# The opening of a two-layer trunk in four even blocks of granules, with eight modulation buffers

## The chip, the cores and the metric

One Trainium2 chip; the kernel runs on one of its cores. The metric is the device time of one execution in microseconds (us), the median of several runs; lower is better. A profiled execution gives the trace from which all rows here come. Engines are named as in the trace: PE is TensorE, DVE VectorE, ACT ScalarE, POOL GpSimd, SP SyncE, which only issues transfers.

## What is computed

A batch of one sequence of 256 tokens, width 2048, float32, goes through two layers. Each layer takes its input, normalizes it, scales and shifts it by a modulation that depends on a condition vector, and adds a gated branch:

```python
cond = jax.nn.silu(c)
for layer in range(DEPTH):                                  # 2
    mod = cond @ ada_w[layer] + ada_b[layer]                # 2048 x 6144 of weights
    shift, scale, gate = jnp.split(mod, 3, axis=-1)
    h = rms_norm(x, norm_w[layer]) * (1.0 + scale[:, None, :]) + shift[:, None, :]
    y = moba_branch(...) if layer % 2 == 0 else mlstm_branch(...)
    x = x + gate[:, None, :] * y
```

Layer 0 is attention: `proj = h @ w_in` gives q, k, v and z of 2048 columns each (16 heads of 128), q and k are normalized and rotated, the attention within one block of 256 tokens is causal, and `(o * silu(z)) @ w_out` is the branch. Layer 1 is an mLSTM of 8 heads. The change concerns the start of layer 0 alone.

## The kernel before

**Precision.** Every weight tile is split on the chip into a high and a low part, and so is h; a product is three matmuls, hi x hi, lo x hi, hi x lo. ACT writes the high part of a weight tile (`hi`, L546, w_hi<-raw), DVE the rest (`lo`, L822, w_lo<-raw,w_hi).

**Granules.** The unit of work on PE is a granule: 256 rows of the contraction (two of 128) by 512 columns of weights, against all 256 tokens. It is 12 matmuls of 128x512 (L1315 to L1317) and uses one weight tile of 512 KB. Tiles lie in LEAD = 5 slots of `raw`, `w_hi`, `w_lo`. A granule is (unit, group, r): the unit is Q, K, V, Z or the output projection O, the group is one of four groups of four heads, r = 0 to 7 is the place in the contraction. Granule r needs the parts 2r and 2r+1 of h, of 16.

**Order.** `ORDER0` lists layer 0's granules. PE runs them in this order; ACT and DVE run the same list with "places": at place i they prepare the tile of granule i + 5 and then do the tasks that a table has for place i (in some tables, `z_copy`, `z_add`, the tasks stand ahead of the preparation). SP issues at place i the load of granule i + 5 and then the modulation tiles that `TAKES0` has for place i. All queues run strictly in order.

**Modulation.** Of layer 0's shift and scale, 16 tiles of 512 KB (128 x 2 x 512) make a block, and four blocks (`b` = 0 to 3) make all; block b yields the modulation of h's parts 4b to 4b+3, thus of r = 2b and 2b+1. A tile is loaded into one of four buffers of `ada_raw` (`load_ada`, L478) and multiplied into a sum by DVE (`take_ada`, L841, a "take"). After 16 takes PE adds up over the partitions (`mod_sum`, L1434, "sum 0" to "sum 3"; it writes bank 3 of `mix`), ACT writes shift and scale (`mod_evac0`, L582 and L585) and makes h: high part L601 and full h L606, two of each for one r (`h_make`); DVE makes the low part (`h_rest`, L887, h_lo). Later tiles (layer 1 and the gates) use the same buffers.

**The opening.** Since h appears in four pieces while the modulation is loaded, the first 56 granules are in four blocks (`BLOCKS0`): 14 with r = 0 and 1, 10 with r = 2 and 3, 16 with r = 2 to 5, and 16 with the rest. To have enough work, the blocks also hold z of groups 0 to 2 and v of group 1 ("z parts"). Q and K of group 0 stay in PSUM banks of their own and V in `mix` 0 and 1; in the first three blocks all z parts take turns in banks 2 and 3 of `mix`. When a part's run in a block ends, ACT copies the bank (`z_copy`, L613) or, if there is a copy from before, DVE adds it (`z_add`, L857). A granule that needs the bank waits for that (`claim0`). Sums 1 to 3 stand behind granules 10, 21 and 36 (`SUM_AFTER`), the last takes of their blocks at places 8, 20 and 35.

**Before the first granule.** SP issues 16 modulation tiles; the four pieces of x come behind tiles 3 (two pieces), 4 and 5. ACT squares x, DVE adds up behind its tenth take, POOL makes the power, ACT and DVE scale x (L566, L873), PE transposes it into eight banks, ACT copies them (L576), and only then PE does sum 0.

The semaphore waits that matter below:

```python
wait(sp, ada_tile, n - ADA_SLOTS + 1)          # load_ada: the buffer's last tile must be taken
wait(sp, lo_ready, number(it, c) - LEAD + 1)   # load_raw
pe.wait_ge(xnT_act, UNIT)                      # ahead of sum 0: all eight banks copied
```

## Time and profile before

| | |
|---|---|
| median of 3 runs | 1515.51 us (1514.44 to 1517.66) |
| the profiled execution | 1514.53 us |
| its span, first to last instruction | 1512.7 us |
| PE busy | 1449.8 us, 96% |
| DVE busy | 1104.8 us, 73% |
| ACT busy | 750.5 us, 50% |
| DMA | 361.47 MB, mean 239 GB/s |
| first granule starts | 46.45 us |

Busy shares are means over the whole span. The opening, up to about 178 us, is another regime than the rest: it is there that the modulation is loaded beside the weights. A duration in the trace is that of one instruction; on PE the next one starts before the last has ended, so the work of a granule is read from the starts. A bracket is idle time of the engine ahead of an instruction, and what ended it.

### The profile page before, as it was taken

To read this page: it belongs to the slowest core of one execution; us is meant where nothing else is said; L and a number is where in the kernel's file an instruction comes from. 1 tells how busy PE (TensorE), PEld (TensorE's weight loads), DVE (VectorE), ACT (ScalarE), POOL (GpSimd) and SP (SyncE) were. 2 spreads that over 40 slices of the span, in tenths; PEclk is the share of its full clock that TensorE was granted. 3 is DMA by queue.
4 is the path that set the end of the run, shared out by engine and by line. 5 is a ranking of instruction groups with operands and counts; after the bars stand their busy time and mean duration, and the time that the engine had idled before them with its cause. 6 is when DMAs were issued, how large, how long until landed. Compare 5 with 4: busy or idle time off the path is not lost.

```text
span 1512.7 us, 19059 instructions
## 1 busy us (share of the span) xinstructions
PE 1449.8 (96%) x6679; PEld 1200.8 (79%) x6679; DVE 1104.8 (73%) x1224; ACT 750.5 (50%) x1024; POOL 42.3 (3%) x78
## 2 busy tenths in 40 slices
PE   2889999999999989999999999999999999999998
PEld 2767888888888867778888888888888888888886
DVE  5889799989989786887866566566666666656657
ACT  3554546455445545645544554454454554454552
POOL 1000010001000000010000000000000000000000
PEclk9899999999999999999999999999999999999999
...
GB/s 312 376 364 367 313 297 339 305 343 269 330 302 351 283 131 181 215 339 289 260 179 193 170 193 184 176 193 182 172 192 191 167 192 190 172 184 193 179 181 112
DMA packets 199230, 361.47 MB, mean 239 GB/s; under 512 B 14224, under 2 KB 48360, under 8 KB 199164
## 3 DMA queue, kind: packets, MB, share of 16 engines
...
q10 hardware_dynamic: 1056, 1.06, 0.2%
...
q14 instruction: 25, 0.20, 0.0%
...
## 4 chain that ended last, share of the span: by engine, by line
PE 76%; issue 9%; DVE 6%; DMA 4%; ACT 3%; SPq 0%; POOL 0%; ACTq 0%; DVEq 0%; POOLq 0%
PE proj L1315 23%; PE proj L1317 22%; PE proj L1316 22%; DVE ada_acc L841 3%; DMA raw<-in_att_w_in 3%; DMA ada_raw<-in_ada_w 2%; PE mix L1315 1%; PE mix L1316 1%; PE mix L1317 1%; DVE w_lo L822 1%; ACT w_hi L546 1%; PE mix L1434 1%; PE mix L1501 1%; PE mix L1549 1%; ACT work L634 1%
## 5 line engine op out<-in xcount | busy, mean ns | idle before, releaser
L822 DVE TENSOR_TENSOR w_lo<-raw,w_hi 128x1024 fp32r<-128x1024 f32 x480 | 586.1, 1223 | 362.2 <-ACT w_hi L546 361.1
L546 ACT ACTIVATE w_hi<-raw 128x1024 fp32r<-128x1024 f32 x480 | 507.8, 1061 | 683.6 <-PE proj L1317 577.5
L1315 PE MATMUL proj<-w_hi,h_hi 128*128 128x512 f32 x1472 | 585.0, 397 | 8.6 <-DVE h_lo L887 5.7
L1317 PE MATMUL proj<-w_hi,h_lo 128*128 128x512 f32 x1472 | 575.7, 391 | 0.0
L1316 PE MATMUL proj<-w_lo,h_hi 128*128 128x512 f32 x1472 | 575.5, 391 | 0.0
L1315 PEld LDWEIGHTS proj<-w_hi,h_hi 128*128 128x128 f32 x1472 | 278.0, 189 | 69.2 <-DVE h_lo L887 6.0
L1317 PEld LDWEIGHTS proj<-w_hi,h_lo 128*128 128x128 f32 x1472 | 277.7, 189 | 58.9
L1316 PEld LDWEIGHTS proj<-w_lo,h_hi 128*128 128x128 f32 x1472 | 278.1, 189 | 57.9 <-issue 1.4
L841 DVE SCALAR_TENSOR_TENSOR ada_acc<-ada_raw,cond,ada_acc 128x1024 f32<-128x1024 f32 x180 | 230.3, 1279 | 10.2 <-DMA ada_raw<-in_ada_w 8.6
L1315 PE MATMUL proj<-w_hi,y_hi 128*128 128x512 f32 x320 | 126.0, 394 | 1.3 <-DVE stream L985 1.3
L1317 PE MATMUL proj<-w_hi,y_lo 128*128 128x512 f32 x320 | 124.6, 389 | 0.0
L1316 PE MATMUL proj<-w_lo,y_hi 128*128 128x512 f32 x320 | 124.5, 389 | 0.0
L1315 PEld LDWEIGHTS proj<-w_hi,y_hi 128*128 128x128 f32 x320 | 60.1, 188 | 14.3 <-DVE stream L985 1.5
L1316 PEld LDWEIGHTS proj<-w_lo,y_hi 128*128 128x128 f32 x320 | 60.1, 188 | 12.8 <-issue 0.5
L1317 PEld LDWEIGHTS proj<-w_hi,y_lo 128*128 128x128 f32 x320 | 60.1, 188 | 12.6
L1315 PE MATMUL mix<-w_hi,h_hi 128*128 128x512 f32 x128 | 51.0, 398 | 4.9 <-issue 4.9
L1316 PE MATMUL mix<-w_lo,h_hi 128*128 128x512 f32 x128 | 50.3, 393 | 0.0
L1317 PE MATMUL mix<-w_hi,h_lo 128*128 128x512 f32 x128 | 50.3, 393 | 0.0
L991 DVE TENSOR_TENSOR ada_raw<-proj,gate 128x1024 f32<-128x1024 f32 x32 | 39.0, 1218 | 5.5 <-PE proj L1317 5.5
L1037 DVE SCALAR_TENSOR_TENSOR work<-work,conv_c 128x256 f32<-128x256 f32 x96 | 40.0, 480 | 0.0
L994 DVE TENSOR_TENSOR stream<-ada_raw,stream 128x1024 f32<-128x1024 f32 x32 | 39.2, 1226 | 1.1
L1315 PEld LDWEIGHTS mix<-w_hi,h_hi 128*128 128x128 f32 x128 | 24.5, 191 | 11.4 <-issue 6.5
(201 smaller groups left out, 902.1 us busy)
## 6 DMA issues: line engine op xcount, KB each, us to landing
...
raw<-in_att_w_in SPq DMA_DIRECT2D x128, 512.0 KB, 7.5
raw<-in_mlstm_w_in SPq DMA_DIRECT2D x128, 256.0 KB, 3.0
...
```

The costliest lines, as they stand in the source:

```text
L546: act.activation(w_hi[:, c % LEAD, :], raw[:, c % LEAD, :], ACT.Copy).then_inc(hi_ready, 1)
L634: op = act.activation(dump0[:, t, h], ps[:, t, h * HD:(h + 1) * HD], ACT.Square, accum_out=qk_ss[:, i:i + 1])
L822: dve.tensor_tensor(w_lo[:, c % LEAD, :], raw[:, c % LEAD, :], w_hi[:, c % LEAD, :].bitcast(F32), ALU.subtract).then_inc(lo_ready, 1)
L841: dve.scalar_tensor_tensor(out=sum_, in0=w, scalar=cond[:, t:t + 1], in1=other, op0=ALU.mult, op1=ALU.add).then_inc(ada_tile, 1)
L991: dve.tensor_tensor(scaled, both[q % 2][:], gate_both(q), ALU.mult).then_inc(out_part, 1)
L994: dve.tensor_tensor(x_q, scaled, x_q, ALU.add).then_inc(out_evac, 1)
L1037: op = dve.scalar_tensor_tensor(out=cv[:, j, :], in0=src, scalar=w, in1=cv[:, j, :], op0=ALU.mult, op1=ALU.add)
L1315: pe.matmul(out_, a_hi, b_hi, start=start, stop=False, **kw)
L1316: pe.matmul(out_, a_hi, b_lo, start=False, stop=False, **kw)
L1317: return pe.matmul(out_, a_lo, b_hi, start=False, stop=stop, **kw)
L1434: op = pe.matmul(mix[bank][:, j:j + 1], ada_acc[:, which, j // 4, j % 4 * P:(j % 4 + 1) * P], ones[:, 0:1], start=True, stop=True)
L1501: op = pe.transpose(mix[2 + f // 2][:, (f % 2) * SEQ + t * P:(f % 2) * SEQ + (t + 1) * P], y[:, t, f * P:(f + 1) * P], ident)
```

## The change

- `BLOCKS0`: four blocks of 14 granules. Block b has r = 2b and 2b + 1 alone, of q, k, v, of z of groups 0 to 2 and of v of group 1. The middle two are written by `middle0`. The sums now stand behind granules 10, 25 and 39, the last takes at places 8, 23 and 37.
- The z parts are thus ended in all four blocks: one copy and three additions each, 12 additions in place of 9 (8 of them ahead of granule 42, where 5 stood ahead of granule 40). The second block begins with a z granule.
- Modulation tiles of layer 0 have eight buffers: four of `ada_raw`, two of a new tensor in space that later tensors of layer 0 use, and two in `work`. To clear that space, `conv_rows` lies in `raw`, and SP waits for its transposes ahead of the first weight tile. From the fifth block on there are four buffers again.
- x is queued one tile earlier (behind tiles 3 and 4).
- `mod_evac0` on ACT (five instructions) is gone; DVE's `mod_evac` (two) does it. For the first r DVE writes the full h (`by_both`) while ACT writes the high part.
- `h_rest` stands ahead of `lo` at its two places, not behind it. Sum 0 waits for four copied banks, not eight.
- The evacuations of q, k, v of group 0 come two places later (43, 45, 47) and so does its attention; it keeps its distance to them.

```diff
+ADA_START = 8
+def middle0(r):
+    both = (r, r + 1)
+    return (unit0(Z_, 0, both) + [(Q_, 0, r)] + unit0(Z_, 1, both) + [(K_, 0, r)] + unit0(Z_, 2, both)
+            + [(V_, 0, r)] + unit0(V_, 1, both) + [(Q_, 0, r + 1), (K_, 0, r + 1), (V_, 0, r + 1)])
...
+            ada_more = opening_only.enter_context(nc.sbuf_tensor("ada_more", [P, 2, 2, NC], F32))
...
-        conv_rows = work[0:TAPS, 4096:8192]
+        conv_rows = raw[:].rearrange("p l n -> p (l n)")[0:TAPS, 0:2 * QK1]
...
+        ada_slot = [ada_raw[:, i] for i in range(ADA_SLOTS)] + [ada_more[:, i] for i in range(2)] + [
+            part(a, 1024, "p (s n) -> p s n", s=2) for a in (5120, 7168)]
...
-        SUM_AFTER = {10: 1, 21: 2, 36: 3}
+        SUM_AFTER = {10: 1, 25: 2, 39: 3}
...
-        Z_ADDS = ((0, 17, z_copied, 1), (1, 20, z_copied, 2), (2, 27, z_copied, 3), (3, 32, z_copied, 4),
+        Z_ADDS = ((0, 15, z_copied, 1), (1, 18, z_copied, 2), (2, 21, z_copied, 3), (3, 24, z_copied, 4),
+                  (0, 29, z_added, 1), (1, 32, z_added, 2), (2, 35, z_added, 3), (3, 38, z_added, 4),
...
-        X_AFTER = {3: [0, 1], 4: [2], 5: [3]}
+        X_AFTER = {3: [0, 1], 4: [2, 3]}
...
-            spans = ((-LEAD, 14, KT), (9, 2, 5), (11, 10, 11), (21, 2, 5), (23, 13, 11), (40, 103, 6 * KT))
+            spans = ((-LEAD, 14, KT), (9, 15, KT), (24, 14, KT), (40, 103, 6 * KT))
...
-            wait(sp, ada_tile, n - ADA_SLOTS + 1)
-            dst = ada_raw[:, n % ADA_SLOTS]
+            wait(sp, ada_tile, n + 1 - (ADA_START if n < ADA_LATE + ADA_SLOTS else ADA_SLOTS))
+            dst = ada_slot[slot_of(n)]
...
+            sp.wait_ge(conv_turned, 1)
             for i in range(-LEAD, NG0 - LEAD):
...
+        def by_both(layer, q):
+            return q % 2 == 1 if layer else q == 0
...
-            dve.wait_ge(h_act, KT * layer + 2 * (q + 1))
-            if layer and q % 2:
+            if by_both(layer, q):
+                if layer:
+                    dve.wait_ge(ht_done, UNIT + q + 1)
+                else:
+                    dve.wait_ge(mod_out, 1)
+                    dve.wait_ge(xnT_act, q + 1)
...
-                for first, sem_, value in ((2, mod_out, 1), (5, z_copied, 1), (8, z_copied, 2), (12, mod_out, 2),
-                                           (16, z_copied, 4), (19, z_added, 1), (24, mod_out, 3), (29, z_added, 3),
+                                           (14, z_copied, 4), (17, z_added, 1), (20, z_added, 2), (23, z_added, 3),
+                                           (28, mod_out, 3), (31, z_added, 5), (34, z_added, 6), (37, z_added, 7),
...
+            pe.wait_ge(xnT_act, 4)
+            mod_sum(pe, 3, 0, 0)
             pe.wait_ge(xnT_act, UNIT)
-            mod_sum(pe, 3, 0, 0)
```

Where instructions moved, first on VectorE around the low part of the first h (L822 and L841 here are lo; L841 and L860 take). Before:

```order
L841 SCALAR_TENSOR_TENSOR ada_acc<-ada_raw,cond,ada_acc 128x1024
L887 TENSOR_TENSOR h_lo<-work,h_hi 128x512
L822 TENSOR_TENSOR w_lo<-raw,w_hi 128x1024
L841 SCALAR_TENSOR_TENSOR ada_acc<-ada_raw,cond,ada_acc 128x1024
L887 TENSOR_TENSOR h_lo<-work,h_hi 128x512
L822 TENSOR_TENSOR w_lo<-raw,w_hi 128x1024
```

and now:

```order
L841 TENSOR_TENSOR w_lo<-raw,w_hi 128x1024
L868 COPY shift_c<-mix 128x4
L869 SCALAR_TENSOR_TENSOR scale_c<-mix,norm_c 128x4
L908 TENSOR_SCALAR work<-stream,scale_c,shift_c 128x256 x2
L913 TENSOR_TENSOR h_lo<-work,h_hi 128x512
L860 SCALAR_TENSOR_TENSOR ada_acc<-ada_raw,cond,ada_bias 128x1024
L860 SCALAR_TENSOR_TENSOR ada_acc<-ada_raw,cond,ada_acc 128x1024
L841 TENSOR_TENSOR w_lo<-raw,w_hi 128x1024
L860 SCALAR_TENSOR_TENSOR ada_acc<-ada_raw,cond,ada_acc 128x1024
```

The copy and the product of `mod_evac` and two operations of full h came in, and the two takes moved behind h_lo.

ScalarE at the same place, between the last copied bank and the first h. Before:

```order
L546 ACTIVATE w_hi<-raw 128x1024
L582 ACTIVATE shift_c<-mix 128x4
L585 ACTIVATE scale_c<-mix,norm_c 128x1 x4
L601 ACTIVATE h_hi<-stream,shift_c,scale_c 128x256
L606 ACTIVATE work<-stream,shift_c,scale_c 128x256
L601 ACTIVATE h_hi<-stream,shift_c,scale_c 128x256
L606 ACTIVATE work<-stream,shift_c,scale_c 128x256
```

and now:

```order
L570 ACTIVATE w_hi<-raw 128x1024
L620 ACTIVATE h_hi<-stream,shift_c,scale_c 128x256 x2
L570 ACTIVATE w_hi<-raw 128x1024
L620 ACTIVATE h_hi<-stream,shift_c,scale_c 128x256
L625 ACTIVATE work<-stream,shift_c,scale_c 128x256
```

The five operations of shift and scale and the two of full h are gone from ahead of the second hi.

VectorE behind sum 1, from lo(15) on. Before:

```order
L822 TENSOR_TENSOR w_lo<-raw,w_hi 128x1024
L841 SCALAR_TENSOR_TENSOR ada_acc<-ada_raw,cond,ada_acc 128x1024 x2
L822 TENSOR_TENSOR w_lo<-raw,w_hi 128x1024
L887 TENSOR_TENSOR h_lo<-work,h_hi 128x512
L841 SCALAR_TENSOR_TENSOR ada_acc<-ada_raw,cond,ada_acc 128x1024 x2
L822 TENSOR_TENSOR w_lo<-raw,w_hi 128x1024
```

and now:

```order
L841 TENSOR_TENSOR w_lo<-raw,w_hi 128x1024
L868 COPY shift_c<-mix 128x4
L869 SCALAR_TENSOR_TENSOR scale_c<-mix,norm_c 128x4
L860 SCALAR_TENSOR_TENSOR ada_acc<-ada_raw,cond,ada_acc 128x1024
L913 TENSOR_TENSOR h_lo<-work,h_hi 128x512
L841 TENSOR_TENSOR w_lo<-raw,w_hi 128x1024
L860 SCALAR_TENSOR_TENSOR ada_acc<-ada_raw,cond,ada_acc 128x1024
L913 TENSOR_TENSOR h_lo<-work,h_hi 128x512
L841 TENSOR_TENSOR w_lo<-raw,w_hi 128x1024
```

`mod_evac` stands behind lo(15), and each h_lo has moved from behind a lo to ahead of it.

## Rows read from the trace of the kernel before

**Rows 1.** Stretches of the opening: length; each engine busy (operations); PEclk; DMA share; GB/s
```profile
0.00:44.00 44.00, 12.45 (x83) 11.96 (x83) 25.05 (x27) 17.99 (x40) 4.02 (x14) 0.98 0.92 312
44.00:83.00 39.00, 34.63 (x144) 28.04 (x145) 35.14 (x31) 21.02 (x25) 0.00 (x0) 0.89 1.05 388
83.00:124.00 41.00, 34.59 (x153) 27.69 (x152) 37.56 (x33) 18.62 (x26) 0.00 (x0) 0.96 1.01 367
124.00:170.00 46.00, 44.87 (x201) 37.05 (x201) 41.06 (x37) 21.00 (x28) 0.00 (x0) 0.96 0.99 354
170.00:218.00 48.00, 48.00 (x220) 39.60 (x220) 40.98 (x49) 28.75 (x65) 8.83 (x5) 1.00 0.83 275
```

**Rows 2.** TensorE in order of time: start us, us, what, idle before it and its releaser
```profile
46.45 0.79 PE L1315 MATMUL proj<-w_hi,h_hi 128*128 128x512 f32 x1 [4.07 <-DVE h_lo L887]
...
71.94 0.47 PE L1315 MATMUL mix<-w_hi,h_hi 128*128 128x512 f32 x1 [0.60 <-issue]
...
81.67 2.08 PE L1434 MATMUL mix<-ones,ada_acc 128*128 128x1 f32 x16 [1.31 <-DVE ada_acc L841]
83.61 0.77 PE L1315 MATMUL mix<-w_hi,h_hi 128*128 128x512 f32 x1
...
89.06 0.47 PE L1315 MATMUL mix<-w_hi,h_hi 128*128 128x512 f32 x1 [1.01 <-issue]
...
95.91 0.50 PE L1315 MATMUL proj<-w_hi,h_hi 128*128 128x512 f32 x1 [1.17 <-DVE h_lo L887]
...
111.94 0.47 PE L1315 MATMUL mix<-w_hi,h_hi 128*128 128x512 f32 x1 [2.13 <-issue]
...
122.44 1.92 PE L1434 MATMUL mix<-ones,ada_acc 128*128 128x1 f32 x16 [2.09 <-DVE ada_acc L841]
...
146.28 0.47 PE L1315 MATMUL mix<-w_hi,h_hi 128*128 128x512 f32 x1 [1.13 <-issue]
```

**Rows 3.** TensorE in order of time, two matmuls at full clock
```profile
101.26 0.39 PE L1317 MATMUL proj<-w_hi,h_lo 128*128 128x512 f32 x1
101.49 0.39 PE L1315 MATMUL mix<-w_hi,h_hi 128*128 128x512 f32 x1
```

**Rows 4.** Waits of SyncE's queue, 0 to 170 us; DMA from 24 to 44 us
```profile
SPq L478 <- DVE ada_acc L841: 93.5, 57, 4.5
...
DMA packets 3347, 6.45 MB, mean 322 GB/s; under 512 B 199, under 2 KB 199, under 8 KB 3347
```

**Rows 5.** ScalarE in order of time: scales, two hi, copy of a z part
```profile
42.49 1.07 ACT L585 ACTIVATE scale_c<-mix,norm_c 128x1 f32<-128x1 f32 x4
...
86.87 1.06 ACT L546 ACTIVATE w_hi<-raw 128x1024 fp32r<-128x1024 f32 x1 [4.24 <-DMA raw<-in_att_w_in]
...
92.95 1.04 ACT L546 ACTIVATE w_hi<-raw 128x1024 fp32r<-128x1024 f32 x1
...
97.14 1.01 ACT L613 ACTIVATE work<-mix 128x1024 f32<-128x1024 f32 x1
```

**Rows 6.** VectorE in order of time, ahead of the first granule: take 11, norm_scale
```profile
30.04 1.28 DVE L841 SCALAR_TENSOR_TENSOR ada_acc<-ada_raw,cond,ada_acc 128x1024 f32<-128x1024 f32 x1 [0.49 <-DMA ada_raw<-in_ada_w]
31.24 1.67 DVE L873 TENSOR_SCALAR work<-stream,stat 128x512 f32<-128x512 f32 x4
```

**Rows 7.** VectorE in order of time: the copy of mod_evac for a later sum
```profile
415.18 0.15 DVE L849 COPY shift_c<-mix 128x4 f32<-128x4 f32 x1
```

**Rows 8.** VectorE in order of time: take, z_add, lo, take; a later lo
```profile
109.43 1.27 DVE L841 SCALAR_TENSOR_TENSOR ada_acc<-ada_raw,cond,ada_acc 128x1024 f32<-128x1024 f32 x1
110.62 1.22 DVE L857 TENSOR_TENSOR work<-mix,work 128x1024 f32<-128x1024 f32 x1
111.76 1.21 DVE L822 TENSOR_TENSOR w_lo<-raw,w_hi 128x1024 fp32r<-128x1024 f32 x1
112.89 1.27 DVE L841 SCALAR_TENSOR_TENSOR ada_acc<-ada_raw,cond,ada_acc 128x1024 f32<-128x1024 f32 x1
...
188.97 1.23 DVE L822 TENSOR_TENSOR w_lo<-raw,w_hi 128x1024 fp32r<-128x1024 f32 x1 [1.37 <-ACT w_hi L546]
```

More of the change, by code:

```diff
@@ L144, in build @@
         h_lo = sb("h_lo", [P, KT, SEQ], F32R)
+        with ExitStack() as opening_only:
+            ada_more = opening_only.enter_context(nc.sbuf_tensor("ada_more", [P, 2, 2, NC], F32))
         y_hi = sb("y_hi", [P, 4, SEQ], F32R)
@@ L327, in build @@
         c_in, conv_turned, norm_turned = (sem(n) for n in ("c_in", "conv_turned", "norm_turned"))
-        norm_out = sem("norm_out")
         raw_in = [ctx.enter_context(nc.semaphore(f"raw_in{i}")) for i in range(LEAD)]
-        ada_in = [ctx.enter_context(nc.semaphore(f"ada_in{i}")) for i in range(ADA_SLOTS)]
+        ada_in = [ctx.enter_context(nc.semaphore(f"ada_in{i}")) for i in range(ADA_START)]
         def wait(eng, sem, value):
@@ L420, in pair0 @@
             elif in_parts(u, g):
-                if r < 6 and not (g == 1 and u == Z_ and r >= 4) or (u, g) == (Z_, 0):
+                if r < 6 or (u, g) == (Z_, 0):
                     return mixes[1]
@@ L458, in load_out, with slot_of, slot_fills @@
             load_raw(sp, it, c, w[:, bass.ds(g * 4 + t0, KG), (q // 2) * NC:(q // 2 + 1) * NC])
+        def slot_of(n):
+            return n % (ADA_START if n < ADA_LATE else ADA_SLOTS)
+        def slot_fills(n):
+            if n < ADA_LATE:
+                return n // ADA_START + 1
+            return ADA_LATE // ADA_START + (n - ADA_LATE) // ADA_SLOTS + 1
         def load_ada(sp, n):
@@ L577, in xnT_evac @@
                            ).then_inc(xnT_act, 1)
-        def mod_evac0(act, b):
-            act.wait_ge(ada_summed, b + 1)
-            act.activation(shift_c[:, 0, 4 * b:4 * b + 4], mix[3][:, 0:4], ACT.Copy)
-            act.wait_ge(norm_out, 1)
-            for kt in range(4 * b, 4 * b + 4):
-                op = act.activation(scale_c[:, 0, kt:kt + 1], mix[3][:, 4 + kt % 4:5 + kt % 4], ACT.Identity,
-                                    scale=norm_c[:, kt:kt + 1], bias=norm_c[:, kt:kt + 1])
-            op.then_inc(mod_out, 1)
+        def by_both(layer, q):
+            return q % 2 == 1 if layer else q == 0
         def h_make(act, layer, q):
@@ L617, in z_silu @@
             for g in range(G0 - 1):
-                act.wait_ge(z_added, 6 + g)
+                act.wait_ge(z_added, 9 + g)
                 act.activation(z0[g], z0[g], ACT.Silu).then_inc(z_ready, 1)
@@ L876, in h_rest @@
         def h_rest(dve, layer, q):
[L878 to L879 removed]
+            if by_both(layer, q):
+                if layer:
[3 more added lines that the diff above has]
+                    dve.wait_ge(xnT_act, q + 1)
                 for k in range(2):
                     kt = 2 * q + k
[L882 to L884 removed]
+                    src = turn_bank(1, q)[:, k * SEQ:(k + 1) * SEQ] if layer else xnT[:, kt, :]
+                    if layer:
+                        dve.wait_ge(h_act, KT + 2 * (q + 1))
+                    op = dve.tensor_scalar(h_full[:, q % 2, k * SEQ:(k + 1) * SEQ], src,
+                                           scale_c[:, layer, kt:kt + 1], shift_c[:, layer, kt:kt + 1], ALU.mult, ALU.add)
                 op.then_inc(h_full_ready, 1)
[L886 removed]
+                dve.wait_ge(h_full_ready, layer + layer * (q // 2) + 1)
+            dve.wait_ge(h_act, KT * layer + 2 * (q + 1))
             dve.tensor_tensor(h_lo[:, 2 * q:2 * q + 2, :].rearrange("p k t -> p (k t)"), h_full[:, q % 2, :],
@@ L1365, in claim0 @@
                 elif g == 1:
-                    pe.wait_ge(z_added, 8 + u)
+                    pe.wait_ge(z_added, 11 + u)
                 else:
@@ L1421, in turn_x @@
                 if q % 2:
[L1422 removed]
+                    pe.wait_ge(h_full_ready, (q - 4) // 2 + 2)
             for k in range(2):
@@ L1482, in pv0 @@
             if g == 1:
-                pe.wait_ge(z_added, 9)
+                pe.wait_ge(z_added, 12)
             else:
```

61 lines of the change are left out of this document (27 added, 34 removed).

## The prediction

> **What bounds the kernel now.** I read first the stretches of the opening [rows 1]: from 170 us on TensorE (PE) is busy all the time, and what it does there is not changed, so only what comes before can shrink. At 44 to 170 us it is busy 114.1 of 126 us with the clock at 0.89 to 0.96, while VectorE (DVE) has 113.8 us of work and the DMA engines are full (388, 367 and 354 GB/s). Three resources are thus near their limit at once, and what one gains the next may take back.
>
> Then the matmuls in order of time [rows 2]. The first granule starts at 46.45, and seven pauses follow, each with its cause: the copy of a z part (71.94), modulation sum 1 waiting for its last tile (81.67), the bank that this sum used (89.06), h_lo (95.91), a z part's addition (111.94), sum 2 waiting for its last tile (122.44), another addition (146.28). The brackets add up to 9.4 us. A matmul lasts 0.39 us but the next starts 0.23 us after it [rows 3], so a pause costs 0.16 us more than its bracket: 7 x 0.16 = 1.1, together 10.5 us. The clock falls to half after each of the first two modulation sums that waited: granule 11 starts at 83.61 and ends 1.01 + 0.16 us before 89.06, so it took 4.3 us where 12 x 0.227 = 2.7 are normal, 1.6 us; the stretch from 124 has 0.96 of 46 us, 1.8 us. In all 10.5 + 3.4 = **13.9 us** lost after the first granule. The third sum waited for nothing and lost no clock.
>
> **Why the sums wait.** SyncE stood 93.5 us in 57 waits for a free modulation buffer [rows 4]. It is one queue, so the raw weights behind that wait are late too: ScalarE (ACT) waits 4.24 us for weights at 86.87 [rows 5], and behind that stand its modulation work and eight operations of h. With four buffers and nothing else in flight the DMA moved only 322 GB/s at 24 to 44 us [rows 4], against 388 in the 39 us after.
>
> **The change, part by part.**
>
> *The first granule.* x is queued one tile earlier, but the norm's sum on VectorE stands behind its tenth take, whose tile is queued where it was, so I take nothing for that. Take 11 no longer waits 0.49 us [rows 6], norm_scale starts about 0.4 us earlier instead of at 31.24 and so does all up to the last turned x: 0.3 us taken. The modulation sum needs four copied banks, not eight; it stands behind the same transposes. The two DVE operations that replace five on ACT take 0.3 us at most (0.15 each [rows 7]) against the 1.07 us of the scales alone [rows 5], but stand behind lo(0): 0.7 us saved. Of the four operations of h (0.49 us each) ACT keeps two and DVE does two beside them: 1.0 us. Sum **2.0 us**: first granule at 44.4. As DVE's takes now stand behind h_lo, it reaches lo(1) at 44.4 + 2 x 1.19 = 46.8 and is done by 48; PE, at half clock, ends granule 0 at 44.4 + 12 x 2 x 0.227 = 49.8. So this costs nothing; without that cover it would cost up to the 2.4 us of the takes.
>
> *Eight buffers.* The last tile of block 1 is the 50th of the queue (4 x, 14 weights, 32 modulation), 26.6 MB with the small rows. Before, 13.7 - 6.45 = 7.3 MB were in at 24 us. At 388 GB/s from there, 26.6 MB are in at 24 + 19.3 / 0.388 = 73.7, with about 1 us to land and the take done at 76. PE comes to sum 1 at 80.2 (81.67 less its pause of 1.5) - 0.8 (pause at 71.94 gone, the weights are earlier) - 2.0 = 77.4: no wait, no clock loss. All four blocks need 111 tiles, 58.9 MB: 24 + 51.6 / 0.388 = 157 us; that is no longer what comes last.
>
> *Blocks of 14, and three more additions.* VectorE's pitches are take 1.19, addition of a z part 1.14, lo 1.13 [rows 8]. A place of lo and take is 2.33 us against PE's 2.72, but a block now has 14 x 2.33 + four additions 4.5 + up to two doubled takes 2.8 + h_lo, sum's result and the rest 1.5 = 41.4 us, against PE's 14 x 2.72 + 2.1 = 40.2. So **VectorE is what comes last in the new opening**. I followed both queues place by place from 77.4 with these pitches. New or remaining waits:
> - granule 12, which needs the bank of sum 1: DVE reads it only behind lo(15), whose weights (54th tile) land at 80.3: 0.7 us;
> - granule 14 is now a z granule directly behind V1's last one, in the same bank, so the copy (1.01 us [rows 5]) lies open, and ACT comes to it behind h and two hi: 1.7 us (1.2 at the least);
> - granule 17 needs the addition at place 15, which DVE reaches 0.7 us too late. Sum 2 then is at 123.5 with four more granules done than at 122.44 before, and its tile (43.6 MB with the small ones, 24 + 36.3 / 0.388 = 118, landed at 119) is there;
> - granules 28 and 29: h_lo is now ahead of lo on VectorE, but the second one still stands behind lo(31), whose hi is behind ACT's eight operations of h (3.9 us: the 6.1 from 86.87 to 92.95 less one hi and the five small operations): 0.4 + 2.5 us;
> - granules 31 and 34 wait for additions: 0.4 + 1.2 us; sum 3 then starts at 168.1, its last addition just done;
> - granule 43, second h_lo of the last block: 0.5 us.
>
> Sum 8.1 us. Each is uncertain by as much as itself: all gone but the copy and three late h_lo of 0.3 us leaves about 2 us; at 2.29 us per addition (what 111.94 cost) they are far more.
>
> *Moved steps.* Attention of group 0 goes two granule places later with the evacuations before it, its output projection does not; nothing is added. VectorE waited 1.37 us at 188.97 [rows 8], so it had caught up there; now it comes there some 1 us later relative to PE. I take nothing for that; between 0 and 1.5 us it could cost. SyncE's new wait for the turned conv_rows stands ahead of all weights; it could cost only if the transposes were later than tile 16's issue, and the copies that need them stand ahead of VectorE's tenth take, so they are done by then: nothing.
>
> **The sum.** 2.0 + 13.9 - 8.1 = 7.8 us. The profiled execution took 1514.5 (span 1512.7), the median of three is 1515.5; from the median 1515.5 - 7.8 = **1507.7**, span about 1504.9.
>
> **A rule against it.** The stretch 44 to 83 shows 388 GB/s for 39 us [rows 1]. The Trainium skill (DMA: Bandwidth & Descriptors, Specifications) gives a limit of about 358 GB/s for the HBM of one core. Were that the ceiling, 58.9 MB would be in at 168 us, sum 3 could start at 170.3, and the sum would give 1509.9. The trace does not agree with it, and by the trace the queue can be fed at 388.
>
> **Rivals.**
> - *DMA no faster than before* (0.20): more buffers don't raise the rate, which stays at 322 to 44 us, 388 to 83, 367 to 124, 354 after [rows 1, 4]. For it: the rate fell in just the stretches where both kinds of tile were in flight. Then sum 1 waits at least 2 us and all of the first granule's gain is gone; sum 2's tile is taken at 83 + 14.7 / 0.367 + 2.2 = 125.3, 1.8 us late, and the clock falls again, 1.8 us. Sum 3 starts 3.6 us later: gain 4.2, **1511.3**. It also holds the limit of the page named above.
> - *Nearly all pauses go* (0.08): only the copy and the late h_lo stay, 2 us: gain 13.9, **1501.6**. Against it: VectorE was idle 12.2 us from 44 to 170 and gets 4 to 5 us more work.
> - *Given back* (0.11): VectorE gets through the opening later than I think, and PE waits for it where before it waited for modulation; two waits at sums and their clock (3.4 us) stay too, and additions cost 1 us each for four of eight more. Gain 0 to 3, **1514**.
> - *Slower* (0.05): each addition costs PE what the one at 111.94 did. One z part's bank is filled again three granules after the last; from the end of a pair to the next use PE has one granule, 2.72 us, the addition takes 1.22, so it decides from 1.5 us of lateness of VectorE. Eight such additions before sum 3 at 2.29 = 18.3 us, and h_lo three times 0.4: 1515.5 - 15.9 + 19.5 = **1519.1**.
>
> **How the numbers follow.** The forecast has 0.56, with a range of its own from 1504.5 to 1510. Range: down to 1501.5 (pauses gone), up to 1512.5, which takes in the DMA case; above it lie most of the last two, 0.15. Two runs of this kernel can be told apart from about 0.2%, 3 us: faster (under 1512.5) 0.56 + 0.20 + 0.08 = 0.84, within 0.11, slower 0.05.
>
> **What would show it.** In the changed profile: the first granule at about 44.4; DMA above 380 GB/s from 24 us on, without SyncE's long waits for modulation buffers; sum 1 near 77.4 and sum 2 near 123.5, no half clock behind them; a pause of 1.2 to 1.7 us before granule 14 that waits for ACT's copy; sum 3 near 168, VectorE over 90% busy from 83 to 168; no pause after granule 43. A wait of sums for tiles with DMA still full would make it the DMA case; pauses that end with z_added, the last two. The forecast would be wrong in its root if VectorE idles for tiles, or if PE waits anew around 210 to 235 us.

## The result, and the profile after

The changed kernel takes **1518.98 us** (median of 11 runs, 1516.94 to 1521.43) against 1515.54 us before (11 runs, 1514.44 to 1518.03) beside it: ratio 1.0021, 95% interval 1.0012 to 1.0030. The forecast was 1507.7 us, and no more than 1512.5. The profiled executions differ by more than the medians: 1520.05 us, span 1518.3, against 1514.53 and 1512.7.

The stretches of the changed kernel; the columns are those of [rows 1], with two stretches more:

```profile
0.00:44.00 44.00, 10.84 (x83) 10.60 (x83) 25.32 (x31) 17.98 (x37) 4.03 (x14) 0.99 0.96 345
44.00:83.00 39.00, 35.78 (x154) 29.19 (x155) 38.36 (x33) 19.33 (x22) 0.00 (x0) 0.94 1.05 384
83.00:124.00 41.00, 39.42 (x170) 31.84 (x169) 37.63 (x36) 19.65 (x24) 0.00 (x0) 0.98 1.05 390
124.00:170.00 46.00, 42.91 (x188) 34.55 (x187) 41.90 (x40) 18.79 (x23) 0.00 (x0) 0.96 0.96 338
170.00:218.00 48.00, 43.48 (x206) 35.71 (x204) 42.95 (x53) 25.32 (x57) 9.55 (x5) 1.00 0.80 273
218.00:240.00 22.00, 21.93 (x99) 18.05 (x100) 18.46 (x24) 13.46 (x26) 0.00 (x0) 0.93 0.98 314
240.00:300.00 60.00, 56.71 (x274) 47.65 (x273) 51.35 (x60) 31.80 (x63) 3.35 (x3) 0.97 0.82 282
```

Up to 124 us it is what was wanted: TensorE busier and at a better clock than in [rows 1]. But from 170 us on, where the kernel before had no pause over 0.4 us until 297, there is now idle time, and two stretches with a clock of 0.93 and 0.97.

TensorE in order of time shows where. These are six of its pauses, each with what ended it (of sum 1 the row shows the first nine of 16 matmuls):

```profile
79.01 1.14 PE L1463 MATMUL mix<-ones,ada_acc 128*128 128x1 f32 x9 [2.04 <-DVE ada_acc L860]
...
92.01 0.47 PE L1343 MATMUL mix<-w_hi,h_hi 128*128 128x512 f32 x1 [1.16 <-issue]
...
138.28 0.50 PE L1343 MATMUL mix<-w_hi,h_hi 128*128 128x512 f32 x1 [2.21 <-DVE h_lo L913]
...
210.00 0.47 PE L1343 MATMUL proj<-w_hi,h_hi 128*128 128x512 f32 x1 [0.54 <-DVE w_lo L841]
...
218.07 0.77 PE L1343 MATMUL proj<-w_hi,h_hi 128*128 128x512 f32 x1 [3.36 <-issue]
...
268.70 1.93 PE L1530 MATMUL mix<-const,work 128*128 128x128 f32 x8 [3.29 <-DVE work L983]
```

(Granules 8, 34 and 43 wait 1.10, 0.80 and 0.69 us besides.) The first three are sum 1, granule 14 and granule 29. The last three stand in the part that I had taken as unchanged: granules 53 and 54, and the transposes of group 0's y (`turn_y`) behind granule 67.

To see where a gain is made and lost, I set the starts of the same granule in two profiles beside each other. The **lead** is the start before less the start in the other kernel, in us. Granule 0 is the first; 380 lies in layer 1. All kernels below are in the table; "opening" says whether the kernel is that of the change up to granule 40.

| kernel | opening | 0 | 12 | 24 | 44 | 52 | 56 | 66 | 70 | 80 | 120 | 380 |
|---|---|---|---|---|---|---|---|---|---|---|---|---|
| after | yes | 2.4 | 3.8 | 11.3 | 4.3 | 6.1 | -0.7 | 0.0 | -5.9 | -6.0 | -6.0 | -5.5 |
| e1 rope behind | yes | 1.9 | 1.8 | 10.0 | 3.2 | 4.9 | -2.0 | -1.3 | -2.1 | -2.3 | -2.3 | -3.5 |
| e12 takes alone | yes | 2.1 | 2.0 | 10.2 | 3.4 | 5.1 | 3.4 | 4.1 | -2.9 | -4.3 | -5.7 | -5.2 |
| e6 both, mild | yes | 2.4 | 3.9 | 12.1 | 6.1 | 7.8 | 6.0 | 6.7 | 5.6 | 1.1 | 1.1 | 1.5 |
| e2 takes later | yes | 2.5 | 2.6 | 10.8 | 4.0 | 5.8 | 4.8 | 5.5 | -2.9 | -2.9 | -15.8 | -16.0 |
| e3 both, strong | yes | 2.4 | 3.9 | 12.0 | 6.0 | 7.7 | 6.8 | 7.5 | 5.5 | 0.0 | -14.8 | -14.1 |
| e9 takes in gaps | yes | 2.0 | 2.0 | 10.2 | 3.4 | 5.1 | 3.3 | 4.0 | -6.2 | -5.0 | -6.6 | -6.5 |
| e11 output clear | yes | 1.8 | 3.5 | 11.4 | 5.4 | 7.1 | 5.3 | 6.1 | 4.5 | 5.4 | -12.9 | -12.3 |
| e7 attention back | yes | 1.5 | 1.4 | 9.6 | 3.7 | -3.5 | -3.1 | -3.1 | -3.1 | -3.1 | -3.1 | -3.9 |
| e8 back and eased | yes | 3.1 | 4.6 | 12.7 | 5.8 | 0.0 | 0.3 | 0.3 | 0.3 | -2.7 | -2.7 | -3.4 |
| e4 before, late | before's | 1.3 | 1.3 | 0.0 | -0.1 | 0.9 | -2.2 | -1.5 | -8.1 | -8.1 | -8.1 | -7.7 |
| e5 four buffers | 4 buffers | 1.4 | 0.6 | 7.5 | 1.5 | 3.3 | -4.8 | -4.1 | -8.4 | -8.4 | -8.4 | -7.9 |
| e10 half takes | less work | 1.9 | 6.1 | 13.0 | 6.0 | 7.7 | 0.9 | 1.6 | -4.4 | -4.4 | -4.4 | -3.9 |

The first row is the story: the opening wins 4.3 us by granule 44, then 5.0 are lost between granules 44 and 56, and 5.2 between 66 and 70. (Some leads hold work that the old order has already done there and the new one has not: the 6.1 at granule 52 holds 1.7 us of transposes, those at granule 66 hold 0.8 us, the transposes of y. So the step from 0.0 to -5.9 is a loss of 5.2, and the same 0.8 goes off in every row whose attention stands two places later. The 11.3 at granule 24 holds sum 2, which now comes four granules later.) The spread of the ten rows with the same opening tells how much of a single profile is chance: 3.2 to 6.1 at granule 44, mean 4.5. Two things make most of it: how long the clock stays low behind sum 1 (the lead at granule 12 is 1.4 to 4.6), and whether it falls behind the wait of granule 29, which costs 1.4 us where it does. It does in six of the ten.

**The first loss.** VectorE of the changed kernel, with the addition (`z_add`) of place 51, for which granule 54 waits:

```profile
206.30 1.23 DVE L953 TENSOR_TENSOR work<-work,stat 128x1024 f32<-128x1024 f32 x1
207.44 1.28 DVE L860 SCALAR_TENSOR_TENSOR ada_acc<-ada_raw,cond,ada_acc 128x1024 f32<-128x1024 f32 x1
...
210.97 1.22 DVE L876 TENSOR_TENSOR work<-mix,work 128x1024 f32<-128x1024 f32 x1
...
216.76 1.21 DVE L876 TENSOR_TENSOR gate<-proj,gate 128x1024 f32<-128x1024 f32 x1
```

and in the kernel before, VectorE at the same addition and TensorE at granule 54:

```profile
219.57 1.22 DVE L857 TENSOR_TENSOR gate<-proj,gate 128x1024 f32<-128x1024 f32 x1
```

```profile
218.68 0.49 PE L1466 MATMUL mix<-work 128*128 128x128 f32 x2 [0.35 <-ACT work L651]
...
222.21 0.47 PE L1315 MATMUL proj<-w_hi,h_hi 128*128 128x512 f32 x1
```

Before, this addition ended at 220.8 and nobody waited: from 218.68 to 222.2 TensorE made group 0's scores, which stood ahead of granule 54. With the attention two places later the scores stand behind granule 55. VectorE has the addition only 2.8 us earlier (216.76 against 219.57), TensorE comes to it 3.6 us earlier (its pause begins at 214.7, the one ahead of the scores began at 218.3) and has no cover: it waits 3.36 us, and the matmuls behind it start 0.43 us apart, half clock, up to 221, 1.4 us more.

**The second loss.** VectorE of the changed kernel, where y of group 0 is made:

```profile
259.43 1.22 DVE L841 TENSOR_TENSOR w_lo<-raw,w_hi 128x1024 fp32r<-128x1024 f32 x1 [1.50 <-ACT w_hi L570]
260.57 1.22 DVE L939 TENSOR_TENSOR work<-work,rope_a 128x1024 f32<-128x1024 f32 x1
...
264.17 1.28 DVE L860 SCALAR_TENSOR_TENSOR ada_acc<-ada_raw,cond,ada_acc 128x1024 f32<-128x1024 f32 x1
265.36 1.22 DVE L841 TENSOR_TENSOR w_lo<-raw,w_hi 128x1024 fp32r<-128x1024 f32 x1
266.50 2.15 DVE L983 SCALAR_TENSOR_TENSOR work<-mix,stat,work 128x128 f32<-128x128 f32 x8
```

and before:

```profile
256.65 2.15 DVE L957 SCALAR_TENSOR_TENSOR work<-mix,stat,work 128x128 f32<-128x128 f32 x8
...
261.04 1.21 DVE L913 TENSOR_TENSOR work<-work,rope_a 128x1024 f32<-128x1024 f32 x1
```

`y0_out` (L983, L957 before) stood at place 63, one place ahead of group 1's first rotation (`rope(dve, 1, 0)`, place 64). It moved to 65 with the attention, the rotation didn't move, and so the two changed order: y now comes behind 3.6 us of rotation and a place of take and lo. `turn_y` waits 3.29 us for it, and loses some 1.7 us of clock behind.

### The profile page after: what moved, and what is told of

It reads as the page before. It is cut to its first block, busy times and chain, and to the rows that moved or that the text cites. A ratio compares the mean times of both kernels' runs of the same rounds, so it can differ in the third digit from the quotient of the medians.

```text
span 1518.3 us, 19062 instructions
## 1 busy us (share of the span) xinstructions
PE 1449.9 (95%) x6679; PEld 1200.3 (79%) x6679; DVE 1108.5 (73%) x1237; ACT 744.5 (49%) x1002; POOL 43.0 (3%) x78
## 4 chain that ended last, share of the span: by engine, by line
PE 73%; issue 11%; DVE 9%; ACT 4%; DMA 2%; SPq 1%; POOL 0%; ACTq 0%; DVEq 0%; POOLq 0%
PE proj L1343 22%; PE proj L1345 22%; PE proj L1344 22%; DVE ada_acc L860 4%; DVE w_lo L841 2%; DMA raw<-in_att_w_in 1%; ACT w_hi L570 1%; PE mix L1343 1%; PE mix L1344 1%; PE mix L1345 1%; DMA ada_more<-in_ada_w 1%; PE mix L1530 1%; ACT h_hi L620 1%; PE mix L1578 1%; ACT work L653 1%
## 5 line engine op out<-in xcount | busy, mean ns | idle before, releaser
L841 DVE TENSOR_TENSOR w_lo<-raw,w_hi 128x1024 fp32r<-128x1024 f32 x480 | 585.5, 1222 | 360.8 <-ACT w_hi L570 359.9
L860 DVE SCALAR_TENSOR_TENSOR ada_acc<-ada_raw,cond,ada_acc 128x1024 f32<-128x1024 f32 x148 | 188.9, 1276 | 2.6 <-DMA ada_raw<-in_ada_w 1.6
L1343 PE MATMUL mix<-w_hi,h_hi 128*128 128x512 f32 x136 | 54.9, 403 | 5.8 <-issue 3.5
L1344 PE MATMUL mix<-w_lo,h_hi 128*128 128x512 f32 x136 | 54.4, 400 | 0.0
L1345 PE MATMUL mix<-w_hi,h_lo 128*128 128x512 f32 x136 | 54.2, 399 | 0.0
```

What stands on the lines that cost most here:

```text
L841: dve.tensor_tensor(w_lo[:, c % LEAD, :], raw[:, c % LEAD, :], w_hi[:, c % LEAD, :].bitcast(F32), ALU.subtract).then_inc(lo_ready, 1)
L860: dve.scalar_tensor_tensor(out=sum_, in0=w, scalar=cond[:, t:t + 1], in1=other, op0=ALU.mult, op1=ALU.add).then_inc(ada_tile, 1)
L1343: pe.matmul(out_, a_hi, b_hi, start=start, stop=False, **kw)
L1344: pe.matmul(out_, a_hi, b_lo, start=False, stop=False, **kw)
L1345: return pe.matmul(out_, a_lo, b_hi, start=False, stop=stop, **kw)
```

## The experiments

All are timed beside the kernel before. "Takes" are the modulation tiles that VectorE adds up.

**e4: the kernel before, with group 0's attention two places later**, and nothing else of the change.

```diff
-                {51: [lambda: turn_qk0(pe, 0, z_added, 6)], 53: [lambda: scores0(pe, 0)],
-                 58: [lambda: turn_p0(pe, 0)], 62: [lambda: pv0(pe, 0)], 65: [lambda: turn_y(pe, 0, y0)]},
+                {53: [lambda: turn_qk0(pe, 0, z_added, 6)], 55: [lambda: scores0(pe, 0)],
+                 60: [lambda: turn_p0(pe, 0)], 64: [lambda: pv0(pe, 0)], 67: [lambda: turn_y(pe, 0, y0)]},
...
-                  56: [lambda: inv0(dve, 0)], 63: [lambda: y0_out(dve, 0)], 65: [lambda: y_lo_dve(dve, 0)],
+                  58: [lambda: inv0(dve, 0)], 65: [lambda: y0_out(dve, 0)], 67: [lambda: y_lo_dve(dve, 0)],
```

> The kernel before with one part of the change alone: group 0's attention two places later (53, 55, 60, 64, 67 on PE, with ScalarE's and VectorE's steps), evacuations, rotation and blocks as they were. Theory A and A2: the opening is untouched, and both later losses appear: scores no longer cover the addition at granule 54 (PE comes 3.5 us earlier than before against 1.4 us of slack: 2 us and clock), and the rotation of group 1 stands ahead of y0 (3 to 3.5 us and clock): 4 to 8 us slower than before, 1520 to 1523. The rival (the later losses come from the opening's own lateness of VectorE): within 1 us of 1515.5.

Measured 1522.21 us (1520.83 to 1523.7) against 1514.96, ratio 1.0044 (1.0031 to 1.0058): 7.3 us slower. The waits are at the two places named (TensorE):

```profile
221.01 0.47 PE L1315 MATMUL proj<-w_hi,h_hi 128*128 128x512 f32 x1 [1.84 <-issue]
...
270.90 1.21 PE L1501 MATMUL mix<-const,work 128*128 128x128 f32 x8 [3.97 <-DVE work L957]
```

So the moved attention alone costs 7.3 us, more than the 3.4 by which the changed kernel is slower. That I priced at 0 to 1.5 us. With the 4.5 us that the opening wins by granule 44, 7.3 leave a loss of 2.8 us, near the 3.4 measured.

**e1: the changed kernel with the rotation behind `y0_out`.**

```diff
-                *[{GROUP0[g] + 8 + (g == 2): [lambda g=g: rope(dve, g, 0)],
+                *[{GROUP0[g] + 8 + (g > 0 and g < 3): [lambda g=g: rope(dve, g, 0)],
```

> The changed kernel with one step moved on VectorE: the rotation of group 1's q one place later, at 65, behind group 0's output y0 and not ahead of it. Theory A (the attention moved by two places ran into group 1's rotation at place 64: 3.6 us of VectorE work now stand ahead of y0_out, PE waits 3.29 us for it at 268.7 and loses about 1.3 us of clock behind that): that wait goes, the kernel is 3.5 to 5 us faster than the changed kernel, about 1514.5. Rival B (VectorE is behind by its whole load and would be as late without that step): the wait stays or comes one step later, time within 1 us of 1519.

Measured 1516.71 us (1512.43 to 1518.23), ratio 1.0003 (0.9993 to 1.0013): 2.3 us less than the changed kernel where 3.5 to 5 were expected. VectorE and TensorE there:

```profile
264.20 2.15 DVE L983 SCALAR_TENSOR_TENSOR work<-mix,stat,work 128x128 f32<-128x128 f32 x8
266.27 1.21 DVE L939 TENSOR_TENSOR work<-work,rope_a 128x1024 f32<-128x1024 f32 x1
```

```profile
266.56 1.04 PE L1530 MATMUL mix<-const,work 128*128 128x128 f32 x8
```

The wait of `turn_y` is gone (no bracket); from granule 66 to 80 its lead falls by 1.0 us where that of the changed one falls by 6.0 (0.8 of both is the transposes of y). So the second loss is this order, shown. The median gives less than that 4.9 us. In the two profiles the difference is partly hidden by an opening that led by 1.1 us less and by 1.2 us that went behind granule 120, in layer 1; why the medians of 11 runs differ by 2.3 us alone is not shown.

**e2 and e3: fewer takes around the z additions**: e2 moves the ten takes of the places 44 to 53 behind them, e3 has e1's edit too.

```diff
-            spans = ((-LEAD, 14, KT), (9, 15, KT), (24, 14, KT), (40, 103, 6 * KT))
+            spans = ((-LEAD, 14, KT), (9, 15, KT), (24, 14, KT), (40, 4, 4), (54, 16, 20), (70, 73, 6 * KT - 24))
```

> The changed kernel with ten modulation takes (for layer 1) moved out of places 44 to 53 to places behind 54. Theory A2 (at granule 54 PE waits for an addition on VectorE, which has no room there, because the scores that stood on PE ahead of this granule and hid VectorE's lateness now stand behind it): VectorE reaches the addition some 10 us earlier, the 0.5 and 3.4 us waits at granules 53 and 54 and about 1.3 us of clock go; 3.5 to 5 us faster than the changed kernel, about 1514.5. Rival B2 (VectorE is paced by ScalarE's high parts and the weights' landing there, not by its own load): less than 1 us. If the takes now crowd places 54 to 70, the wait at y0 grows.

> Both moves together, the rotation behind y0 and the ten takes behind place 54. If the two losses are independent, as the theory has it, the gains add up: 7 to 10 us faster than the changed kernel, 1509 to 1512, which beats the kernel before (1515.5) by what the opening alone gains (4.7 us by granule 43 in the trace). If they are one and the same lateness of VectorE, together they give no more than the larger one, about 1514.5.

Measured 1531.43 us for e2 (ratio 1.0104, 1.0088 to 1.0119) and 1528.71 us for e3 (1.0085, 1.0071 to 1.0099): both far from what was expected. Yet the waits at granules 53 and 54 are gone, and e3 still leads by 5.5 us at granule 70. The time goes later, where I had not counted how many takes each sum needs. Two pauses of e3:

```profile
359.86 2.45 PE L1463 MATMUL mix<-ones,ada_acc 128*128 128x1 f32 x16 [2.66 <-DVE ada_acc L860]
...
416.86 3.54 PE L1463 MATMUL mix<-ones,ada_acc 128*128 128x1 f32 x16 [4.27 <-DVE ada_acc L860]
```

These are sums 6 and 7, behind granules 95 and 110. Sum 6 needs 48 takes after place 40; the edit left 49 by place 94, and VectorE was not there in time. A test of one place had broken a condition at another.

**e6 and e12: only the takes of the places 48 to 53 moved**, most of them into 54 to 94, so that sum 6 has 51 by place 94, one less than in the changed kernel; e6 with e1's edit, e12 without it.

```diff
-            spans = ((-LEAD, 14, KT), (9, 15, KT), (24, 14, KT), (40, 103, 6 * KT))
+            spans = ((-LEAD, 14, KT), (9, 15, KT), (24, 14, KT), (40, 8, 8), (54, 41, 43), (95, 48, 45))
```

> The changed kernel with its late attention, the rotation of group 1 behind y0_out, and 5 takes moved out of the places 48 to 53 as in the run beside this one. The stronger version of it (10 takes moved, the later places too full) led before by 7.5 us at granule 66, and lost it all behind granule 94, where sums 6 and 7 waited for their takes. Theory: with the deadlines kept some of this lead stays: 1512 to 1514 us. Rival (five more takes behind 54 delay y0_out, y_lo and the later steps as in the stronger version): 1515 to 1519 us.

> The changed kernel with the evenly moved takes alone (5 of the takes at the places 48 to 53 moved to 54 to 94); the rotation of group 1 stays ahead of y0_out. Theory (two separate losses: the queue ahead of the z additions at granule 54, and the rotation ahead of y0_out at 68): the pause and the low clock at granule 54 go as in the run with both, the turn of y waits as in the changed kernel, or more, since takes now stand ahead of y0_out too: the lead over before is 6 us at granule 66 and gone by granule 70; 1518 to 1521 us. Rival (one common delay, which the moved takes cure alone): no wait at the turn of y, 1515 us as with both.

e6: **1515.04 us** (12 runs, 1512.24 to 1518.45) against 1515.72, ratio 0.9998 (0.9989 to 1.0006). e12: 1518.46 us (1516.38 to 1519.82), ratio 1.0015 (1.0006 to 1.0024). The addition ahead of granule 54 now stands at 211.41 in e6, and e6 has neither of the two losses: it leads by 5.6 us at granule 70. e12 has the second alone:

```profile
264.63 1.97 PE L1530 MATMUL mix<-const,work 128*128 128x128 f32 x8 [3.29 <-DVE work L983]
```

That is the same 3.29 us as in the changed kernel. So there are two losses with two causes, each cured by its own edit; the rival of one common delay falls. But e6 loses 4.5 of its 5.6 us by granule 80, in the middle of what the first output projection needs:

```profile
291.07 2.67 DVE L860 SCALAR_TENSOR_TENSOR ada_acc<-ada_raw,cond,ada_acc 128x1024 f32<-128x1024 f32 x2
293.65 1.22 DVE L1011 TENSOR_TENSOR stream<-proj,stream 128x1024 f32<-128x1024 f32 x1
```

```profile
294.92 0.50 PE L1343 MATMUL proj<-w_hi,y_hi 128*128 128x512 f32 x1 [3.80 <-DVE stream L1011]
```

VectorE comes to the output step of place 75 (L1011) only behind the second rotation, a lo and three takes, and TensorE waits 3.80 us for it at granule 78, 2.5 us more than the 1.31 us of the kernel before there, with 1.6 us of half clock behind it.

**e9 and e11: that wait too.** Both have e1's edit. e9 puts the moved takes into gaps of VectorE (two at each of the places 57 to 59, 62 and 63, three in all at 74 to 79). e11 has e6's spread up to place 72 and none at 73 to 75; its edit is:

```diff
-            spans = ((-LEAD, 14, KT), (9, 15, KT), (24, 14, KT), (40, 103, 6 * KT))
+            spans = ((-LEAD, 14, KT), (9, 15, KT), (24, 14, KT), (40, 8, 8), (54, 19, 20), (76, 4, 4),
+                     (80, 15, 16), (95, 15, 16), (110, 33, 32))
```

> The changed kernel with the rotation of group 1 behind y0_out, and its takes fitted into VectorE's idle stretches: none at the places 48 to 53 (where the turn and the z additions of group 0 are queued), two at each of 57 to 59, 62 and 63 (where VectorE was idle for some 3 us at a time), three in all at 74 to 79 (where the second rotation of group 1 and the first output steps are queued), with each sum finding its takes in time. The run with the evenly moved takes led before by 5.2 us at granule 76 and lost 4.1 of them at granules 78 to 80, where TensorE waited for VectorE's output step. Theory (VectorE's order alone costs the lead): this wait goes, the lead of 5 us stays to the end: 1510 us, between 1508 and 1513. Rival (the doubles at 57 to 63 delay y0_out, or the wait only moves behind granule 80): 1514 to 1517 us, as the evenly moved ones.

> The run with the evenly moved takes and the rotation behind y0_out, with one more edit: no take at the places 73 to 75 (20 at 54 to 72, 4 at 76 to 79, 16 at 80 to 94, 16 at 95 to 109, 32 behind), so that VectorE's output step at 75, for which TensorE waited 2.1 us at granule 78 and ran 1.9 us at the low clock behind it, comes some 3 to 4 us earlier; every sum still has its takes in time, sums 6 and 7 just so. Theory (VectorE's order around group 0's attention and the first output steps costs the lead, and nothing else does): the wait at granule 78 goes, the lead of 5 us at granule 76 stays, and the time is 3 to 4 us below the evenly moved one's 1515.0: 1511 to 1512 us, the first version to beat before. Rival (VectorE is full from 54 on, so each stretch that is cleared fills another): a new wait at sums 6 or 7, at g96 or g111, or at y0_out, of 2 to 5 us with the clock: 1514 to 1518 us.

e9: 1522.09 us (1520.22 to 1524.81), ratio 1.0046 (1.0032 to 1.0059). e11: 1526.87 us (1525.87 to 1528.6), ratio 1.0075 (1.0061 to 1.0089). The waits are where the rivals put them, but both times lie above even the rivals' ranges, 1514 to 1517 and 1514 to 1518. TensorE of e9 at `turn_y`, then of e11 at sums 6 and 7:

```profile
267.88 1.97 PE L1531 MATMUL mix<-const,work 128*128 128x128 f32 x8 [6.49 <-DVE work L984]
```

```profile
356.86 3.54 PE L1464 MATMUL mix<-ones,ada_acc 128*128 128x1 f32 x16 [5.00 <-DVE ada_acc L861]
...
414.98 3.54 PE L1464 MATMUL mix<-ones,ada_acc 128*128 128x1 f32 x16 [4.29 <-DVE ada_acc L861]
```

e11's wait at granule 78 is gone and it still leads by 5.4 us at granule 90, the best of all kernels there. Then it lacks the takes: 48 are queued by place 94 where 51 were, and that is 5 us late. Between places 54 and 110 VectorE has so little room that each of the stretches cleared here filled another with a deadline of its own. My theory that only the order mattered falls for this stretch.

**e7 and e8: the attention back at before's places**, in the changed kernel; e8 with e6's takes.

```diff
-                {53: [lambda: turn_qk0(pe, 0, z_added, 9)], 55: [lambda: scores0(pe, 0)],
-                 60: [lambda: turn_p0(pe, 0)], 64: [lambda: pv0(pe, 0)], 67: [lambda: turn_y(pe, 0, y0)]},
+                {51: [lambda: turn_qk0(pe, 0, z_added, 9)], 53: [lambda: scores0(pe, 0)],
+                 58: [lambda: turn_p0(pe, 0)], 62: [lambda: pv0(pe, 0)], 65: [lambda: turn_y(pe, 0, y0)]},
```

> The changed kernel with group 0's attention put back to the places of before: turns of q and k after granule 51, scores after 53, the turn of p after 58, p times v after 62, the turn of y after 65, with the steps of ScalarE and VectorE that belong to them; only the two rotations stay at 44 and 47, since q and k are complete two granules later. Theory (the later attention is the whole loss: 7.7 us in the kernel before, where it was moved alone): the scores stand ahead of granule 54 again and cover its z addition, and y0_out stands ahead of the rotation of group 1, so both waits (some 2.9 and 4.8 us with the clock) go, and the lead of 4 to 6 us that the opening has at granule 52 reaches the end: 1511 us, between 1509 and 1514. Rival (the attention was moved because its inputs come later): the turn after 51 waits for the second rotation and for the z addition at 49, some 2 to 4 us, and the clock falls with it: 1515 to 1517 us, no better than before.

> The attention back at its places as in the run with that alone, and 5 of the modulation takes moved from VectorE's places 48 to 53 to the places 54 to 94 (8 takes at 40 to 47, 43 at 54 to 94, 45 at 95 to 142), so that sums 5, 6 and 7 find their takes. Theory (VectorE is full around the places 48 to 54, and what is queued there delays the turn and the z additions): 1 to 2 us less than with the attention back alone, 1509 to 1511 us. Rival (VectorE is full over the whole stretch from 54 to 70 too, so the takes only move the wait to y0_out, y_lo or a sum): same time or up to 4 us more.

e7: 1518.6 us (1515.92 to 1519.85), ratio 1.0016 (1.0007 to 1.0025). e8: 1519.26 us (1517.58 to 1522.0), ratio 1.0030 (1.0019 to 1.0041). TensorE of e7 at the transposes of q and k behind granule 51, and VectorE's addition that they need:

```profile
212.85 3.65 PE L1483 MATMUL mix<-const,work 128*128 128x128 f32 x16 [5.51 <-issue]
```

```profile
211.54 1.22 DVE L876 TENSOR_TENSOR work<-mix,work 128x1024 f32<-128x1024 f32 x1
```

The rival's mechanism is right: this addition (place 49) is queued behind the rotation of k, which comes two granules later with the new blocks. `turn_y` waits no more, but the 5.5 us here and the half clock behind them take 6.8 us of lead by granule 56, and the median is only 0.4 us below the changed kernel's. In e8, with fewer takes ahead, the same wait is 4.35 us and the lead is 0.3 us at granule 56; then granule 78 waits 2.75 us, with half clock behind. So in the blocks of 14 neither version could put the attention back without a wait of 4 us and more. That no arrangement of VectorE's queue would allow it isn't shown.

**e5: the changed kernel with four modulation buffers.**

```diff
-ADA_START = 8
+ADA_START = 4
```

> The changed kernel with four modulation buffers in place of eight, everything else as changed. Theory (VectorE, not the transfers, bounds the time to sum 1 once there are eight buffers; with four SyncE's queue waits for takes again, as 93.5 us of its waits in the kernel before): the weights behind those waits come late as before, the pauses at granules 5, 12 and 19 come back in part, and the time is 3 to 6 us more than the changed kernel's, 1522 to 1525 us. Rival (the eight buffers do nothing, since VectorE is continuous from 43 to 79 us whatever they are): 1519 us, no change.

Measured 1523.05 us (1522.52 to 1525.56), ratio 1.0053 (1.0040 to 1.0066): 4.1 us above the changed kernel, as expected. The pause comes at granule 5:

```profile
63.65 0.76 PE L1343 MATMUL mix<-w_hi,h_hi 128*128 128x512 f32 x1 [2.76 <-issue]
```

**e10: the changed kernel with half of each of 15 takes left out.**

```diff
-            dve.scalar_tensor_tensor(out=sum_, in0=w, scalar=cond[:, t:t + 1], in1=other,
+            cut = slice(0, NC if KT < n < 2 * KT else 2 * NC)
+            dve.scalar_tensor_tensor(out=sum_[:, cut], in0=w[:, cut], scalar=cond[:, t:t + 1], in1=other[:, cut],
```

> The changed kernel in which 15 of the 16 takes that sum 1 waits for add only the first 512 of their 1024 columns, which leaves out half of the modulation's second block; the transfers are unchanged. Theory (VectorE, continuous from 43.3 to 78.9 us, sets sum 1, since its backlog of lo parts and takes outlasts the transfers): some 15 x 0.5 = 8 us less of VectorE work ahead of the sum, so the wait of 2.0 us and the 1.7 us of low clock behind it go, granule 12 starts at about 81.5 instead of 85.2 us. Rival (the transfers set it): sum 1 starts at 79 us as before. What arrives at the end is less than what is gained, since the later waits for the scores and y0_out catch it: 1516 to 1519 us.

Measured 1518.19 us (1516.5 to 1519.31), ratio 1.0018 (1.0009 to 1.0027). Sum 1, with no wait:

```profile
76.80 1.92 PE L1464 MATMUL mix<-ones,ada_acc 128*128 128x1 f32 x16
...
82.98 0.47 PE L1344 MATMUL mix<-w_hi,h_hi 128*128 128x512 f32 x1 [1.41 <-issue]
```

With the same tiles to load sum 1 comes 2.2 us earlier and the clock stays: VectorE set it, not the transfers. Granule 12 then waits 1.4 us for the bank, the wait I had forecast at 0.7. The medians moved by 0.8 us only: 1.7 us more lead at granule 44, which is within the spread of the openings above (e6 and e3 have 6.0 too), and then the same two losses.

## Why the prediction was wrong, point by point

- *First granule at 44.4*: right, 44.08, and 44.2 on the mean of the ten kernels with this opening. The clock also came back sooner behind it: the lead grows from 2.4 to 3.9 us by granule 2 (by 1.2 us on the mean of the ten), a term that I did not have.
- *Eight buffers*: the transfers did as forecast. The DMA's line from 24 to 44 us, and SyncE's waits up to 170 us (the columns of [rows 4], which had 322 GB/s and 93.5 us):

```profile
DMA packets 4080, 7.86 MB, mean 393 GB/s; under 512 B 242, under 2 KB 242, under 8 KB 4080
```

```profile
SPq L444 <- DVE w_lo L841: 74.9, 39, 5.5
SPq L501 <- DVE ada_acc L860: 16.1, 21, 2.1
```

  The Trainium skill (DMA: Bandwidth & Descriptors, Specifications) gives about 358 GB/s as the limit of one core's HBM, half of what the two cores of a stack share. With one core at work this trace does not agree with it either: 393 GB/s here and 390 from 83 to 124 us.

  What failed is the step from there to sum 1. I put the last take at 76, from the rate of the DMA alone, and followed VectorE's queue only from 77.4 on. But SyncE now waits for VectorE's lo, which frees the weight buffers: VectorE works without a gap from 43.29 to 78.86 and its last take of block 1 ends there.

```profile
75.25 1.28 DVE L860 SCALAR_TENSOR_TENSOR ada_acc<-work,cond,ada_acc 128x1024 f32<-128x1024 f32 x1
76.45 1.22 DVE L841 TENSOR_TENSOR w_lo<-raw,w_hi 128x1024 fp32r<-128x1024 f32 x1
77.58 1.28 DVE L860 SCALAR_TENSOR_TENSOR ada_acc<-work,cond,ada_acc 128x1024 f32<-128x1024 f32 x1
79.12 1.23 DVE L841 TENSOR_TENSOR w_lo<-raw,w_hi 128x1024 fp32r<-128x1024 f32 x1 [0.26 <-ACT w_hi L570]
```

  From [rows 8]: 16 takes, 13 lo and two h_lo are 16 x 1.19 + 13 x 1.13 + 2 x 0.6 = 34.9 us, so from 43.3 the take could not be done before 78. The same sum as for the later blocks, and not made here. It costs 2.2 us and 1.7 of clock. e10 shows it: without that work, sum 1 stands at 76.8, without a wait.
- *The eight waits of the new order*: 8.1 us forecast. Measured, each as a step longer than 0.23 us: granule 12 none (0.7), 14 1.3 (1.7), 17 0.6 (0.7), 28 and 29 0.2 and 2.4 (0.4 and 2.5), 31 and 34 none and 1.0 (0.4 and 1.2), 43 0.8 (0.5): 6.3 us, so these were well sized. Not in my list: granule 8, 1.3 us (the copy of a z part is queued behind a hi that waits for its weights), and 1.8 us of low clock behind granule 29. In this execution the clock fell behind a wait of 2.2 us for h_lo just as behind a sum; I had charged it for sums alone. With sum 1 that is 13.3 us.
- So the opening wins 4.3 us by granule 44, 4.5 on the mean of ten, where 7.8 were forecast. By the terms: 2.4 (granule 0) + 1.5 (the clock behind it) + 13.9 - 13.3 = 4.5. Sums 2 and 3 came without a wait, as forecast, and e5 puts 4.1 us on the buffers.
- *Moved steps: "nothing is added"*. **This step turned the sign.** I looked whether VectorE was late at 188.97, and not what the moved steps had covered, nor what they now stood behind. Two lookups would have shown both: the scores stood between the end of granule 53 and granule 54, while the addition for granule 54 ended at 220.8 in the trace of before, 1.4 us ahead of its use; and the rotation's place, 64, lies between 63 and 65. e4 measured the step: 7.3 us in place of 0 to 1.5.
- *Rivals*: "given back", 1514 us, was right that little of the gain would last, but by the opening, not behind it. By its number the case slower, 1519.1, is almost the 1518.98 measured, and that is luck: it was made of eight additions of the opening at 2.29 us each, and in the changed kernel only two of them are waited for, 0.6 us at granule 17 and 1.0 at granule 34; the addition that cost most is at granule 54, behind the opening. I had written that a new wait around 210 to 235 us would prove the forecast wrong in its root; it is there, and I gave it no chance of its own.
- The share left for slower, 0.05, was too small for a change that moves a dozen steps of a queue that was continuous from 190 to 228 us.

The lead that is made in the opening can be kept up to granule 76 (e6, 5.2 us) and even to 90 (e11, 5.4 us), but no version here carries it through the sums behind. The best, e6, is no faster than before by its interval. Whether a version with the sums 6 and 7 placed later would do it was not tried. e6's median is 0.7 us below that of the kernel before, its profile 1.5; its twelve executions spread over 6 us, so the difference of two profiles says little here.
